# Two more raw weight buffers for the folded pairs, their low part 6 made by VectorE, and the order of some copies

## What is computed

```python
x = LN1(alpha*x + 0.5*SwiGLU_1(x))                        # hidden width 2816
x = LN2(alpha*x + W_mix_out[conv_group(x) | dsa_group(x)])  # sparse attention, top 256 keys
x = LN3(alpha*x + MemCrossAttn(x, mem))                   # 4 heads, 256 memory tokens
x = LN4(alpha*x + 0.5*SwiGLU_2(x))
# SwiGLU(x) = (silu(x @ w_gate) * (x @ w_up)) @ w_down
```

## Time and profile before

| | us |
|---|---|
| median of 3 runs (2554.87 to 2562.17) | 2558.52 |
| the profiled execution | 2561.5 |
| its span, first to last instruction | 2559.6 |
| PE busy | 2437.2 (95%) |
| PE weight loads busy | 2207.8 (86%) |
| POOL busy | 1358.8 (53%) |
| DVE busy | 1047.2 (41%) |
| ACT busy | 1030.1 (40%) |
| mean granted PE clock, as a share of full speed | 0.985 |

### The profile page before, as it was taken

How to read it: one execution, slowest core, us unless ns; L and a number is a source line. 1 busy time by engine, 2 the same in 40 slices (tenths; PEclk the granted TensorE clock), 3 DMA queues, 4 the chain that set the end, 5 groups by cost and what they waited for, 6 DMA issues and landing times.

```text
span 2559.6 us, 40246 instructions
## 1 busy us (share of the span) xinstructions
PE 2437.2 (95%) x16095; PEld 2207.8 (86%) x16095; DVE 1047.2 (41%) x1981; ACT 1030.1 (40%) x1877; POOL 1358.8 (53%) x878
## 2 busy tenths in 40 slices
PE   8999999999999999998999999999899997988997
PEld 8888889889999999986889878888579897988997
DVE  1000003265800004377443889993545245342323
ACT  4333333433333334455353523332654445444341
POOL 4776665534666665422344767766106254646463
PEclk9999999999999999998999999999999998999999
DMA  4444532443232232533122233333302222423232
GB/s 148 119 117 122 159 91 80 138 148 101 83 97 86 87 87 80 152 91 121 38 67 67 75 90 108 108 91 99 131 34 71 62 59 75 120 78 107 75 100 68
DMA packets 425664, 245.01 MB, mean 96 GB/s; under 512 B 23008, under 2 KB 415328, under 8 KB 424720
## 3 DMA queue, kind: packets, MB, share of 16 engines
q1 hardware_dynamic: 389712, 197.88, 27.0%
q10 hardware_dynamic: 33200, 32.56, 4.0%
q0 software_dynamic: 2576, 12.07, 1.2%
HBM read 218.79 MB, written 21.74 MB: 94 GB/s over the span
## 4 chain that ended last, share of the span: by engine, by line
PE 74%; DVE 6%; POOL 6%; ACT 5%; DMA 4%; issue 3%; ACTq 0%; DVEq 0%; SPq 0%; POOLq 0%
PE LIN L984 66%; DMA WRAW<-in_ffn_up 3%; POOL WL L2504 2%; PE TR L1328 1%; POOL WL L2510 1%; PE LIN L1061 1%; ACT WH L1380 1%; PE TR L1037 1%; POOL FP L2525 1%; POOL XL L2587 1%; ACT PR L1915 1%; PE LIN L1276 1%; ACT PT L1940 1%; PE TR L1138 1%; DVE SC L2115 1%
## 5 line engine op out<-in xcount | busy, mean ns | idle before, releaser
L2504 POOL TENSOR_TENSOR WL<-WRAW,WH 128x1024 fp32r<-128x1024 f32 (+1 forms) x342 | 802.5, 2349 | 457.2 <-ACT WH L1380 452.1
L984 PE MATMUL LIN<-XH,WH 128*128 128x256 f32 (+3 forms) x2456 | 721.2, 325 | 21.1 <-DVE Y L2183 6.4
L984 PE MATMUL LIN<-XH,WL 128*128 128x256 f32 (+3 forms) x2456 | 713.8, 322 | 0.0
L984 PE MATMUL LIN<-XL,WH 128*128 128x256 f32 (+3 forms) x2456 | 713.4, 322 | 0.0
L984 PEld LDWEIGHTS LIN<-XH,WH 128*128 128x128 f32 (+1 forms) x2456 | 438.8, 189 | 62.0 <-issue 19.7
L984 PE MATMUL LIN<-HH,WH 128*128 128x256 f32 (+2 forms) x1632 | 466.4, 308 | 8.3 <-POOL HL L2530 7.1
L984 PEld LDWEIGHTS LIN<-XL,WH 128*128 128x128 f32 (+1 forms) x2456 | 438.4, 189 | 33.9
L984 PEld LDWEIGHTS LIN<-XH,WL 128*128 128x128 f32 (+1 forms) x2456 | 436.7, 189 | 33.8
L984 PE MATMUL LIN<-HL,WH 128*128 128x256 f32 (+2 forms) x1632 | 463.3, 306 | 0.0
L984 PE MATMUL LIN<-HH,WL 128*128 128x256 f32 (+2 forms) x1632 | 462.8, 306 | 0.0
L1380 ACT ACTIVATE WH<-WRAW 128x1024 fp32r<-128x1024 f32 (+2 forms) x346 | 355.7, 1030 | 130.3 <-DMA WRAW<-in_ffn_gate 30.7
(11 more groups left out here) (239 smaller groups left out, 3154.9 us busy)
## 6 DMA issues: line engine op xcount, KB each, us to landing
WRAW<-in_ffn_gate SPq DMA_DIRECT2D x88, 512.0 KB, 3.8
WRAW<-in_ffn_up SPq DMA_DIRECT2D x88, 512.0 KB, 3.8
WRAW<-in_ffn_down SPq DMA_DIRECT2D x64, 512.0 KB, 3.7
WRAW<-in_w_mix_in SPq DMA_DIRECT2D x44, 512.0 KB, 3.8
WRAW<-in_ffn_down SPq DMA_DIRECT2D x32, 384.0 KB, 3.3
WRAW<-in_w_mix_out SPq DMA_DIRECT2D x16, 512.0 KB, 3.6
WRAW<-in_w_mem_q SPq DMA_DIRECT2D x16, 512.0 KB, 3.6
WRAW<-in_w_mem_o SPq DMA_DIRECT2D x16, 512.0 KB, 3.6
```

The source lines that it names most:

```text
L984: last = pe.matmul(LIN[0:pr.rows, pr.slot, out:out + w], wt[:, SLOT[pr.tile], c, 0:pr.rows], x[:, c, col:col + w], start=(c == 0 and wt is ...
L2504: pool.tensor_tensor(WL[:, SLOT[n], 0:nk, 0:width], WRAW[:, n % 2, 0:nk, 0:width], WH[:, SLOT[n], 0:nk, 0:width].bitcast(F32), ALU.subtrac ...
```

## The change

- Raw buffers: WRAWX, two more, over KIP and what follows it (free in this feed forward). Pairs of odd q use them, pairs of even q and all other tiles WRAW as before. `raw_places` gives each tile its buffer (RAW_AT), its turn in it and the tile that lay there before (RAW_BEFORE), for which its load waits. A load into WRAWX by a pair not preceded by a pair four tiles back waits for the last product of the memory output.
- Low part 6 goes from POOL to DVE (`up_low`), at the head of DVE's `fold` ahead of L2056, and for the pairs that follow plain tiles behind the product before. It has a semaphore of its own, up_lo.
- ACT copies PB ahead of HH.
- POOL, behind a part's last pair, does the low parts of two down tiles, then FP and HL, then the other two.
- TH and TL are made one at a time behind products 4, 5 (these two run together), 6 and 7 instead of two behind 5 and two behind 6.
- "gains" goes from ahead of pair 0's work to ahead of pair 3's. YT and YOUT move within their region by 2688 bytes.

The replacements of WRAW[:, n % 2] by raw(n) in the split functions, and the declarations of semaphores, are left out here.

```diff
@@ -383,15 +383,18 @@
         norm_strands(memo, ffn, norm + 1, True)
         if folded(2, g):
             ffn[RING].mid.append(("fold sums",))
-            ffn[RING + 1].end.append(("fold highs", 0))
-            ffn[RING + 2].end.append(("fold highs", 2))
+            for k in range(4):
+                ffn[RING + k].end.append(("fold part", k))
             for k in range(KD // 2):
                 ffn[2 * RING + k].end.append(("scale", k))
         if g.index == 0:
             ffn[2 * RING].mid.append(("select", 1))
             ffn[20].end.append(("tails",))
         else:
-            ffn[2 * RING].mid.append(("gains",))
+            if folded(2, g):
+                [pr for pr in ffn if isinstance(pr, Pair) and pr.part == 0][-1].mid.append(("gains",))
+            else:
+                ffn[2 * RING].mid.append(("gains",))
             for t in range(4):
                 if folded(2, g):
                     [pr for pr in ffn if pr.kind == "down" and pr.part == t // 2][1 + 2 * (t % 2)].end.append(("early", t))
@@ -457,6 +460,20 @@
 
 
 IN_PAIR, SLOT, COUNT, LAST_OF, FOLLOWS = tile_places()
+
+
+def raw_places():
+
+
+    place, turn, before, held, times = {}, {}, {}, [None] * 4, [0] * 4
+    for k in range(NT):
+        at_ = k % 2 + (2 * (IN_PAIR[k].q % 2) if k in IN_PAIR else 0)
+        times[at_] += 1
+        place[k], turn[k], before[k], held[at_] = at_, times[at_], held[at_], k
+    return place, turn, before
+
+
+RAW_AT, RAW_TURN, RAW_BEFORE = raw_places()
 
 
 def reads_before():
@@ -578,8 +595,10 @@
         CMKT = place("CMKT", [P, KD, N_MEM], F32, r_sc + 8192)
         MKTS = place("MKTS", [P, KD, N_MEM], F32, r_sc)
         MVS = place("MVS", [P, 2, D], F32, r_sc + 8192)
-        YT = place("YT", [P, 2, KD, P], F32, r_sc)
-        YOUT = place("YOUT", [P, 2, D], F32, r_sc + 8192)
+        r_yt = r_sc + SCORE_COLS * 4 - 16384
+        assert r_kip + 8192 <= r_yt
+        YT = place("YT", [P, 2, KD, P], F32, r_yt)
+        YOUT = place("YOUT", [P, 2, D], F32, r_yt + 8192)
 
         r_a = region(8704)
         r_b = region(10240)
@@ -616,6 +635,7 @@
         TL = place("TL", [P, 4, 4, FS], F32R, r_kpa + 16 * FS * 4)
         assert r_kpa + 32 * FS * 4 <= r_kip
         TF = place("TF", [P, 4, 4, FS], F32, r_kpa + 16 * FS * 4)
+        WRAWX = place("WRAWX", [P, 2, KD, P], F32, r_kip)
         PA = place("PA", [P, 2, FS], F32, r_a + 3 * GC * 4)
         PB = place("PB", [P, FS], F32, r_b + 4 * GC * 4)
 
...
@@ -769,11 +789,14 @@
             k = i - 1
             return TR[:, k // 2, 512 * (k % 2):512 * (k % 2) + 512]
 
+        def raw(n):
+            return (WRAW if RAW_AT[n] < 2 else WRAWX)[:, RAW_AT[n] % 2, :, :]
+
         def raw_part(two, up, half):
-            return WRAW[:, (two.tile + up) % 2, 4 * half:4 * half + 4, :]
+            return raw(two.tile + up)[:, 4 * half:4 * half + 4, :]
 
         def raw_here(engine, n):
-            engine.wait_ge(raw_loaded[n % 2], (n // 2) * 16 + 16)
+            engine.wait_ge(raw_loaded[RAW_AT[n]], 16 * RAW_TURN[n])
 
         def block_free(engine, two, i):
 
@@ -860,14 +883,21 @@
         @block.sync
         def _(sp):
             for n, (name, c0, width, row, nk) in enumerate(PLAN.weights):
-                if n >= 2 and n - 2 in IN_PAIR:
-                    two = IN_PAIR[n - 2]
+                before = RAW_BEFORE[n]
+                if before in IN_PAIR:
+                    two = IN_PAIR[before]
                     sp.wait_ge(sum_ready, 4 * two.q + 4)
-                    sp.wait_ge(plain_lo, 3 * two.q + (2 if n - 2 == two.tile else 3))
-                elif n >= 2:
-                    sp.wait_ge(lo_split, COUNT[n - 2])
-                sp.dma_start(WRAW[:, n % 2, 0:nk, 0:width], weight[name][:, row:row + nk, c0:c0 + width])\
-                    .then_inc(raw_loaded[n % 2], 16)
+                    if before == two.tile:
+                        sp.wait_ge(plain_lo, 2 * two.q + 2)
+                    else:
+                        sp.wait_ge(up_lo, two.q + 1)
+                elif before is not None:
+                    sp.wait_ge(lo_split, COUNT[before])
+                if RAW_AT[n] >= 2 and (n < 4 or n - 4 not in IN_PAIR):
+
+                    sp.wait_ge(product, [pr for pr in PLAN.products if pr.name == "memo"][-1].p + 1)
+                sp.dma_start(raw(n)[:, 0:nk, 0:width], weight[name][:, row:row + nk, c0:c0 + width])\
+                    .then_inc(raw_loaded[RAW_AT[n]], 16)
 
 
             for k, t in enumerate(FINAL):
@@ -893,8 +923,10 @@
                 first = not isinstance(two.before[0], Pair)
 
                 def half_product(i, out, hi, lo, start, fresh=None):
-                    if i in (0, 5, 6):
-                        pe.wait_ge(plain_lo, 3 * q + (1, 2, 3)[(0, 5, 6).index(i)])
+                    if i == 6:
+                        pe.wait_ge(up_lo, q + 1)
+                    elif i in (0, 5):
+                        pe.wait_ge(plain_lo, 2 * q + (1, 2)[(0, 5).index(i)])
                     else:
                         pe.wait_ge(sum_lo, 4 * q + i)
                     if fresh is not None:
...
@@ -1420,10 +1452,10 @@
                 if q:
                     act.wait_ge(part_summed, 3 * q)
                 act.activation(PA[:, 0, 0:w], chain, ACT.Copy).then_inc(part_copied, 1)
+                act.wait_ge(part_done, 7 * q + 2)
+                act.activation(PB[:, 0:w], sum_bank(w), ACT.Copy, scale=0.5).then_inc(part_copied, 1)
                 if isinstance(two.before[0], Pair):
                     hidden_high(two.before[0])
-                act.wait_ge(part_done, 7 * q + 2)
-                act.activation(PB[:, 0:w], sum_bank(w), ACT.Copy, scale=0.5).then_inc(part_copied, 1)
                 act.wait_ge(part_done, 7 * q + 3)
                 act.activation(PA[:, 1, 0:w], chain, ACT.Copy).then_inc(part_copied, 1)
                 for s in range(2):
@@ -1738,11 +1770,10 @@
                     store_early(t)
                     if t + 2 < EARLY:
                         load_y(t + 2)
-                elif kind == "fold highs":
-                    w = current[0].cols // 2
-                    for k in range(what[0], what[0] + 2):
-                        act.wait_ge(fold_summed, 4 * FOLDED.index((2, current[0].index)) + k + 1)
-                        act.activation(TH[:, k, :, 0:w], TF[:, k, :, 0:w], ACT.Copy).then_inc(fold_hi, 1)
+                elif kind == "fold part":
+                    w, k = current[0].cols // 2, what[0]
+                    act.wait_ge(fold_summed, 4 * FOLDED.index((2, current[0].index)) + k + 1)
+                    act.activation(TH[:, k, :, 0:w], TF[:, k, :, 0:w], ACT.Copy).then_inc(fold_hi, 1)
                 elif kind == "scale":
                     g = current[0]
                     act.wait_ge(fold_summed, 4 * FOLDED.index((2, g.index)) + 4)
...
@@ -2025,6 +2056,12 @@
                 dve.tensor_tensor(block_of(two, WL, i), folded_weight(i).rearrange("p (c n) -> p c n", c=4),
                                   block_of(two, WH, i).bitcast(F32), ALU.subtract).then_inc(sum_lo, 1)
 
+            def up_low(two):
+
+                dve.wait_ge(plain_hi, 3 * two.q + 3)
+                dve.tensor_tensor(block_of(two, WL, 6), raw_part(two, 1, 1), block_of(two, WH, 6).bitcast(F32),
+                                  ALU.subtract).then_inc(up_lo, 1)
+
             def ahead_of_pair(n):
 
                 following = follower(n)
@@ -2043,6 +2080,7 @@
                     sum_low(following, 3)
                 if s == 3:
                     sum_low(following, 4)
+                    up_low(following)
 
             def fold(two):
                 w, q = two.g.cols // 2, two.q
@@ -2050,6 +2088,8 @@
                 on = isinstance(following, Pair)
                 if two.part:
                     dve.wait_ge(added, ADDED_AT[two.which, two.g.index] + KD * two.part)
+                if isinstance(two.before[0], Pair):
+                    up_low(two)
                 dve.wait_ge(multiplied, two.event - 1)
                 dve.wait_ge(part_done, 7 * q + 4)
                 dve.wait_ge(part_copied, 4 * q + 3)
@@ -2085,14 +2125,13 @@
                 dve.wait_ge(fold_summed, k0 + 2)
                 dve.tensor_tensor(t[3], b21, t[1], ALU.subtract).then_inc(fold_summed, 1)
 
-            def fold_lows(first):
+            def fold_low(k):
                 g = current[0]
                 w, k0 = g.cols // 2, 4 * FOLDED.index((2, g.index))
                 dve.wait_ge(fold_summed, k0 + 4)
-                for k in range(first, first + 2):
-                    dve.wait_ge(fold_hi, k0 + k + 1)
-                    dve.tensor_tensor(TL[:, k, :, 0:w], TF[:, k, :, 0:w], TH[:, k, :, 0:w].bitcast(F32), ALU.subtract)\
-                        .then_inc(fold_lo, 1)
+                dve.wait_ge(fold_hi, k0 + k + 1)
+                dve.tensor_tensor(TL[:, k, :, 0:w], TF[:, k, :, 0:w], TH[:, k, :, 0:w].bitcast(F32), ALU.subtract)\
+                    .then_inc(fold_lo, 1)
 
```

(19 more changed lines are left out.)

5 lines of the change are left out of this document (2 added, 3 removed).

## The result

The changed kernel takes 2517.03 us (median of 4, 2513.08 to 2520.49) where the kernel before takes 2559.85 beside it: ratio 0.9835, 95% interval 0.9814 to 0.9856. Measured again on another occasion it was 0.9848 (0.9834 to 0.9861). Forecast were 2519.3 (2511 to 2533) and a ratio of 0.985.

A forecast was written before the change was run, and what follows sets the result against it. TensorE, 74% of the chain, bounds the kernel, with 53.2 us of waits and slow clock; terms 8.4 - 1.5 + 3.2 + 15.0 + 5.5 + 8.6 = 39.2 us gained give 2519.3 us, range 2511 to 2533.

The forecast's parts named there:

- The ring: Each steady pair: low part 6, up tile's issue, landing, sums, L2061, half product 6; TensorE waits in it, 2.3 us a pair.
- the ties: Pairs 4 to 17: L2014's hold and ScalarE's PA finish about when TensorE needs them; 0.2 us lost a pair, 0 to 0.75.
- rival B: Pairs: up_low goes before FP, or L2014 is held longer; 0.75 lost a pair instead of 0.2, 2527 us; chance 0.17.
- Rival C: Waits go but the slow clock stays elsewhere: five more falls at 1.7 us each, +8.5, 2528 us; chance 0.11.
- the excess: Exit behind pair 11: 66.70 us against 61.2 for 487 matmuls at 0.1257; it bounds the gain to 5.5.
- the gains' transfers beside down 2: Exit behind pair 3: four transfers share the DMA engines with down 2, so 0.5 to 2.0 us of wait stays.
- Pair 0: Pair 0 with the wait before it: 5.5 of 13.9 us remain, 8.4 gained.
- The term for PA: Pair 0: TensorE's 2.58 us wait for PA; PA comes 1.8 sooner and 0.9 stays.
- the 1.8 of slow clock: Right behind the wait before pair 0: the clock still falls to 0.58, and the 1.8 us lost there stays.
- The term for pair 3: Pair 3: the gains' issues on top of the scalings hold PA, 2.7 us (1.9 to 3.3), plus 0.8 of slow clock.
- My own sign for it: Pair 3: a gap before half product 2 of over 1.5 us would show the forecast right.
- The slower rival: Pairs: each two-input DVE instruction waits out a whole GpSimd instruction, 3.5 us a pair instead of 2.3; 2567 us, chance 0.04.

The follow-up runs named there:

- the port order run: GpSimd starts low part 0 of the next pair only after VectorE's first sum, against the kernel with scalings moved and token parts spread further; 0.9822 of the kernel before.
- The run with the old order: GpSimd makes three down tiles' low parts ahead of FP and HL behind a part's last pair, against the changed kernel; 0.9871 of the kernel before.

## Why the prediction was right, step by step

- The ring was the bound. Four buffers alone took 27.8 of 43.4 us off, and two buffers put back 25.2.
- Pairs 4 to 10: forecast 15.0 gained, measured 90.29 - 74.70 = 15.6; pairs 12 to 17 8.6, measured 9.3. The 0.2 a pair for the ties was 0.16 in eight of these thirteen pairs and nothing in the other five, and the port order run shows it to be the hold of L2014's successor by low part 0, forecast at +0.39 and measured at 1.23 - 0.70 = 0.53. FP was at work ahead of up_low wherever the two met, so rival B didn't come; the margin was 0.10 to 0.13 in the steady pairs and 0.04 to 0.06 in pairs 1 to 3, and no run here shows what a flip would cost.
- Rival C didn't come either: no fall of the granted clock between pair 1 and pair 17 (1.00 in five rows, 0.96 to 0.98 before).
- Behind pair 11: forecast 5.5, measured 6.5; the 4.24 is gone. The 5.5 was "bounded by the excess", and the excess was too small: I had priced all 487 matmuls at 0.1257, but 16 of them are transposes of 128 columns, and the changed kernel does the same 487 in 60.24 us, not 61.2. Behind pair 3: forecast 3.2 with 0.7 left, measured 4.0 with 0.36 left. The run with the old order shows the step that did it. What I had put down for the gains' transfers beside down 2 (0.5 to 2.0) didn't come: that tile was issued at 2188.38 and landed in 3.3 us. Down tiles 4 and 5 came late for ScalarE, but not for TensorE.
- Pair 0: forecast 8.4, measured 24.72 - 17.34 = 7.4. The term for PA was mis-sized: 0.9 was to stay and 2.06 did. And the 1.8 of slow clock ahead of it was no term of its own: with a clock that doesn't fall the wait is 2.55 and pair 0 as long (14.27 to 14.28 in three kernels). The two together were to leave 2.7 over 84 matmuls and left 3.7, since PA came 1.0 sooner and not 1.8 (S + 7.22 before, S + 6.21 now). I had GpSimd's FP there at its old length (0.98), but it came at the same time as VectorE's low part of the tokens:

```profile
2144.41 1.28 DVE L2133 TENSOR_TENSOR TL<-TF,TH 128x1088 fp32r<-128x1088 f32 x1
```

```profile
2144.40 1.96 POOL L2663 TENSOR_TENSOR FP<-FG 128x288 f32<-128x288 f32 x1
```

It ended at 2146.36, 0.67 behind TL's end (2145.69), and HH, block 6, TH 3 and PA followed it. FG was ready 1.0 sooner than before, and FP ended at S + 4.31 as before: the hold took the gain back. This is read from the trace; no run keeps the two apart. I had weighed the port for VectorE in the pairs, and hadn't carried it to GpSimd at this place.
- Pairs 1 to 3: forecast a loss of 1.5, measured a gain of 0.65. The term for pair 3 was mis-sized: 2.7 for the gains' issues, measured 0.64 of wait, as in pairs 1 and 2 (0.85 with its restart), and no fall of the clock, for which 0.8 stood. My own sign for it, a gap of over 1.5 in pair 3, failed too. The issues went out from 2180.09 to 2182.25, while ScalarE worked through copies that wait for nothing:

```profile
2180.96 0.57 ACTq L1624 DMA_DIRECT2D YT<-spill_y  x1
2181.07 0.41 ACT L1471 ACTIVATE FG<-LIN 128x272 f32<-128x272 f32 x1
2181.35 0.65 ACT L1419 ACTIVATE WH<-WRAWX 128x512 fp32r<-128x512 f32 x1
2181.56 0.69 ACTq L1624 DMA_DIRECT2D YT<-spill_y  x1
2181.87 1.22 ACT L1784 ACTIVATE Y<-Y 128x544 f32<-128x544 f32 x2
2182.96 0.41 ACT L1454 ACTIVATE PA<-LIN 128x272 f32<-128x272 f32 x1
```

- Sum: forecast 39.2, in the folded stretch 43.4, between the medians 42.8. The misses are 1.0 at pair 0 one way, 2.2 at pairs 1 to 3 the other, and 3 us of small ones (0.6 to 1.0 in each of the other stretches). The mechanism held; that the total is only 4 off owes something to the first two cancelling in part.
- The slower rival (port exclusion in full) is excluded by the same rows: of three two-input instructions two are held, by 0.53 and 1.1, and one of these has 1.9 to spare.

## What to carry to other kernels

Draw the ring through the buffer that a load waits for (last reader, issue, landing, first reader, and back) and compare it with the work it feeds: here 12.5 against 10.56. The second pair of buffers, which opens it, was worth six times what the earlier last reader was (25.2 against 4.0 us), and with the ring closed the earlier issue mostly came back as a later landing. Once such a ring is open, what is left here are places where VectorE reads two SBUF operands beside GpSimd: order the two by a semaphore, the one on the short path first. The four DMA issues cost ScalarE nothing where it had copies queued that needed no wait, and put work that has slack behind the copy that TensorE waits for, not ahead of it. And don't add the slow clock behind one wait to the next wait: where another engine sets the time of the next matmul, the slow stretch runs inside that wait.
